# The single dense group of a tick moved from behind the prompt's scores to behind the transposes

## The reference, cut to what matters

```
h  = RMSNorm(x) * (1 + a1) + s1                       # modulation from silu(c) @ w_ada
q, k, v, hc, B, C, ga, gb = h @ w_in
beta = sigmoid(q.k / 8 + b_h)                          # 8 heads x 64
A[t,s] = beta[t,s] * prod_{s<j<t} (1 - beta[t,j])      # stick breaking, strictly causal
y  = B * dwconv3_causal(C * hc)
x  = x + g1 * (sigmoid(ga) * (A v @ w_att_out) + sigmoid(gb) * (y @ w_conv_out)) @ w_o
x  = x + g2 * relu(h2 @ w_mlp1)^2 @ w_mlp2             # h2 = RMSNorm(x) * (1 + a2) + s2
```

## Time and profile before

| | |
|---|---|
| median of 3 runs | 1692.57 us (1691.83 to 1693.04) |
| the profiled execution, its own time | 1693.47 us |
| its span, first to last instruction | 1691.7 us |
| mean granted clock of TensorE | 0.995 of full speed |
| TensorE busy, matmuls | 1648.2 us (97%) |
| VectorE busy | 870.2 us (51%) |
| GpSimd busy | 598.9 us (35%) |
| ScalarE busy | 371.2 us (22%) |
| middle stage | from 195.6 to 742.0 us of the span |

### The profile page before, as it was taken

The page is one execution under the profiler, slowest core; times in us unless marked ns, Lnnn a source line. Parts: engine busy times, 40 slices in busy tenths (PEclk is TensorE's granted clock), DMA queues, the critical chain, the costliest instruction groups (busy, mean ns, idle before and its releaser), DMA issues.

```text
span 1691.7 us, 29977 instructions
## 1 busy us (share of the span) xinstructions
PE 1648.2 (97%) x11976; PEld 1534.8 (91%) x11976; DVE 870.2 (51%) x1381; ACT 371.2 (22%) x702; POOL 598.9 (35%) x344
## 2 busy tenths in 40 slices
PE   6999999999999999999999999999999999999999
PEld 5898788878788788899999899999999999999998
DVE  5554364564554454438743865454554555454543
ACT  5344222222222222231111522020202011110200
POOL 0345143333343333313243143443443343343342
PEclk8999999999999999999999999999999999999999
DMA  9013346566566666425321011111111111111112
GB/s 379 27 51 100 139 163 225 201 200 215 198 213 222 207 220 230 150 103 204 127 102 50 26 50 51 50 38 51 51 38 51 50 39 49 50 45 44 51 39 102
DMA packets 71932, 194.63 MB, mean 115 GB/s; under 512 B 8018, under 2 KB 8147, under 8 KB 71795
## 3 DMA queue, kind: packets, MB, share of 16 engines
q1 hardware_dynamic: 67394, 178.62, 30.6%
q10 hardware_dynamic: 4400, 14.10, 2.2%
HBM read 174.26 MB, written 18.42 MB: 114 GB/s over the span
## 4 chain that ended last, share of the span: by engine, by line
PE 90%; DVE 3%; POOL 2%; DMA 1%; ACT 1%; issue 1%; SPq 1%; ACTq 0%; POOLq 0%; DVEq 0%
PE bank L655 78%; PE bank L805 2%; PE bank L780 2%; PE bank L793 2%; PE bank L829 2%; PE bank L853 1%; PE bank L685 1%; POOL wl L592 1%; DMA pre<-in_weights 1%; DVE h2L L1550 1%; POOL wh L590 1%; DVE hL L1269 1%; DVE sc L1582 1%; DMA ring<-in_cache_v 0%; DVE xt L1278 0%
## 5 line engine op out<-in xcount | busy, mean ns | idle before, releaser
L590 POOL TENSOR_TENSOR wh<-raw,zero 128x1024 fp32r<-128x1024 f32 x84 | 160.7, 1913 | 637.4 <-PE bank L655 637.4
L592 POOL TENSOR_TENSOR wl<-raw,wh 128x1024 fp32r<-128x1024 f32 x114 | 281.2, 2467 | 110.4 <-ACT wh L1069 103.8
L655 PE MATMUL bank<-hH,wh 128*128 128x352 f32 x832 | 277.2, 333 | 1.3 <-POOL wl L592 0.8
L655 PE MATMUL bank<-hL,wh 128*128 128x352 f32 x832 | 268.0, 322 | 0.0
L655 PE MATMUL bank<-hH,wl 128*128 128x352 f32 x832 | 267.5, 322 | 0.0
L655 PE MATMUL bank<-h2H,wh 128*128 128x352 f32 x768 | 249.2, 325 | 4.0 <-DVE h2L L1550 3.0
L655 PE MATMUL bank<-hidH,wh 128*128 128x352 f32 x768 | 247.7, 323 | 0.0
L655 PE MATMUL bank<-h2H,wl 128*128 128x352 f32 x768 | 246.9, 321 | 0.0
L655 PE MATMUL bank<-h2L,wh 128*128 128x352 f32 x768 | 246.7, 321 | 0.0
L655 PE MATMUL bank<-hidH,wl 128*128 128x352 f32 x768 | 246.3, 321 | 0.0
L655 PE MATMUL bank<-hidL,wh 128*128 128x352 f32 x768 | 246.1, 320 | 0.0
(11 more groups left out here) (177 smaller groups left out, 2571.3 us busy)
## 6 DMA issues: line engine op xcount, KB each, us to landing
raw<-in_weights SPq DMA_DIRECT2D x152, 512.0 KB, 3.5
ring<-in_cache_k SPq DMA_DIRECT2D x128, 256.0 KB, 3.9
ring<-in_cache_v SPq DMA_DIRECT2D x128, 256.0 KB, 3.6
pre<-in_weights SPq DMA_DIRECT2D x16, 512.0 KB, 15.9
gate_scratch<-gt ACTq DMA_DIRECT2D x14, 528.0 KB, 3.4
act<-gate_scratch SPq DMA_DIRECT2D x14, 528.0 KB, 5.1
xt<-in_xT SPq DMA_DIRECT2D x8, 528.0 KB, 6.9
act<-in_xT SPq DMA_DIRECT2D x8, 528.0 KB, 4.4
```

Source lines behind the costliest of these rows:

```text
L590: mark(pool.tensor_tensor(wh[u % 2][:, :], src[:, :], zero[:, 0:1].to_broadcast([P, 1024]), ALU.add))
L592: pool.tensor_tensor(wl[u % 2][:, :], src[:, :], wh[u % 2][:, :].bitcast(F32), ALU.subtract)\
L655: mm = pe.matmul(out, x, y, start=n == 0, stop=n == end)
```

## The change

The two conditions in `ticks()` are swapped. Group B is now there in every tick, and group A only where there are two. The number of groups in every tick and their order stay as they were; only in the 18 single ticks does the one group go from place A to place B, on TensorE as on the engines that read it or split its weights. The eviction and the split of such a tick move with it, and so do the keys by which loads are sorted.

```diff
@@ -219,10 +219,10 @@
     g, m, n = MIX0, 0, 16
     end = PLAN.phase["merge"][0]
     for k in range(TICKS):
-        if g < end:
+        if g < end and (k % 8 in (0, 1, 3, 4, 6) or k >= NSTEP):
             DENSE_A[k] = g
             g += 1
-        if g < end and (k % 8 in (0, 1, 3, 4, 6) or k >= NSTEP):
+        if g < end:
             DENSE_B[k] = g
             g += 1
         if k % 4 != 3 and m < NITEM:
```

## The result

The changed kernel takes 1726.19 us (median of 5 runs, 1723.49 to 1729.17) against 1692.57 us before: 2.0% slower, a ratio of 1.020 with a 95% interval of 1.0186 to 1.0214. The forecast was 1721.5 us with a range of 1711 to 1731. The profiled execution took 1724.13 us, with a span of 1722.3 us, 30.6 us more than before. Its mean granted clock is 0.989; before it was 0.995.

What follows compares the result with a forecast made beforehand. TensorE's matmuls were taken to bound the kernel, with time lost where its queue stands still. Costs of 36.6 less 9.4 plus 1.7 for the clock make 28.9 us: 1693.47 to 1722.4, less 0.9, 1721.5 us; range 1711 to 1731.

Steps and rivals of the forecast that it cites:

- Transposes held by VectorE's copy: Single ticks with sample turn: transposes wait for VectorE's sample copy behind the scans; 3.25 us each in six 512-key ticks.
- only the sigmoids count: Rival, chance 0.07: in single ticks VectorE's copy does not hold the transposes, only ScalarE's sigmoids do; 7.6 us, 1700 us.
- Ada turn held by the sigmoids: Single ticks: TensorE's ada turn waits for ScalarE's second sigmoid, 2.59 us after the start with 512 keys.
- The waiting in sum: Middle stage: single ticks cost 36.6 us gross, 9.4 of stalls before values and sample values go away, net 27.2.
- The clock: Middle stage: TensorE's bare stretches bring one more fall to half clock than now, net 1.7 us.
- add up to more than two or three: Sign in the changed trace: the forecast is wrong if windows at half clock exceed this count.
- The rival that gave the clock 13.6: Chance 0.13: the clock falls in most bare single ticks, eight falls at 1.7 us; 1733.4 us in all.
- Moved eviction and split: Single ticks: eviction and weight split go later with the group; priced at 0, between -1 and +2 us.

Runs made afterwards that it cites:

- the copy first: Changed kernel with VectorE taking modulation and sample copy ahead of 1 - beta and the scans in the 18 single ticks; 1699.61 us, ratio 1.0042 to the kernel before.
- filled kernel: Changed kernel plus 184 matmuls that nothing reads, put into the bare waits of 16 single ticks; 1714.53 us, ratio 1.0132 to the kernel before.
- fitted cut: Changed kernel with 2 to 7 of 8 row blocks before the transposes in 16 single ticks, the rest behind; 1683.56 us, again 1684.32 us.
- kernel with both remedies: Changed kernel with 3 of 8 row blocks in front in 16 single ticks, and modulation and sample copy ahead of VectorE's scans; 1686.97 us, ratio 0.9971.

## Why the prediction came out as it did

The direction, the place and the mechanism were right, and the time is in the range. Two terms of the sum were off in opposite directions, the clock the more, so that the nearness of the number is partly luck.

- *Transposes held by VectorE's copy.* Right. Predicted start with 512 keys 5.78, found 5.60; line 1388 is the releaser of 17.8 us; putting the copy first moved the start to 3.97. The rival "only the sigmoids count" is what that kernel makes true, and it measured 1699.6 where the rival's sum said 1700. In the changed kernel it is excluded.
- *Ada turn held by the sigmoids.* Right: predicted at 2.59 with 512 keys, found 222.53 - 220.05 = 2.48, since TensorE goes on 0.05 behind the sigmoid and not 0.15.
- *The waiting in sum.* Predicted 36.6 gross and 9.4 back, 27.2. By groups the changed kernel waits 18.8 + 12.8 + 1.6 = 33.2, and 8.9 + 0.5 + 1.5 = 10.9 went away, the last of them already in front of the transposes; that is 22.3. The filled kernel gives 22.5. So the sum was 4.9 too dear. Most of that can be found tick by tick. In the twelve ticks with a sample turn the transposes start earlier than worked out, 2.2 in sum: I set the sample copy 0.20 behind the end of the scans, and in tick 2 it starts at 225.22, 0.03 behind their end at 225.19. Tick 21 was priced by tick 45, whose old start is 5.68; its own was 6.54, another 0.9. The ada turns of ticks 15, 23, 39 and 47 wait 3.7 for 4.3. The rest is not broken down. Ticks 13 and 37 went the other way: without modulation their old start is 0.18 earlier, but the new one is not, which the prediction had assumed.
- *The clock.* The mis-sized term. The prediction counted by the one fall of before and took "one more than now net, 1.7", though it saw two bare stretches in a tick of 512 keys. The changed kernel has eight half-speed pieces. They cost 11.1 us in the profiled execution, 9.5 net of the 1.6 that the one fall cost before; the filled kernel puts it at 10.2 by times. The prediction had also named this as a sign of being wrong: windows at half clock that "add up to more than two or three". By that sign its clock term failed. The rival that gave the clock 13.6 was nearer in this term, though with its 27.2 us of waiting it comes out at 1733.4, too high.
- *Why the clock fell.* No single wait of TensorE in the stage is above 2.61 us, the clock went down and up six times, and with the waits filled it did not fall. The page that the prediction cites (the Trainium skill, TensorE: Matmul & The Clock Gate, "A second HAM failure mode: psum-queue depth-cycling") puts such a back and forth down to frequent short idle times between groups of matmuls. The traces agree with it.
- *The sum.* Waiting 22.3 and clock 9.5 make 31.8 of the 32.1 us by which the stage is longer. Behind the stage it is 1.5 us less: there the kernel before had one more fall (a granted clock of 0.53 from 968.0 to 971.6 us) and the changed one none. Together 30.6, the difference of the spans. Predicted 28.9, from 27.2 and 1.7: 4.9 too much waiting hid more than half of the 7.8 us that were missing for the clock.
- *Moved eviction and split.* Priced at 0. The double ticks of the changed kernel keep their lengths, 13.01 us in tick 9, 11.92 in tick 36, as before; only tick 35 is 1.6 shorter, which is the fall that it had before. Whether the order of single loads matters was not tried.

## What to carry to other kernels

A piece of work that fills a wait should be judged by what lies beside it on all other engines, not by what waits behind it: here 3.84 us of matmuls hid a chain of 5.6 us in front to save stalls of 0.5 us on average behind. If both places need cover, cut the piece to fit: 6 of 8 blocks in front in the ticks of 512 keys, 2 to 7 in the others (none in ticks 7 and 31), made the kernel 0.55% faster than the one before. When a change opens idle stretches on TensorE, add the falls of its clock to the sum; here they were a third of the loss, and filling the stretches with matmuls that nothing reads measured them.

## What was not expected of the hardware

- *Matmuls that nothing reads made a kernel faster.* 184 more matmuls, 10.2 us less time, on the same chip, with the granted clock of the stage at 1.00 in place of 0.98.
- *Run-to-run spread goes with the clock.* Runs of the changed kernel differ by 6.6 us, in step with the mean granted clock (0.990 to 0.986), and those of the kernel before by 6.7 (0.999 to 0.994). The filled kernel and the copy first lie within 1.7 us, but with 4 and 5 runs, and the fitted cut, with shorter idle stretches than the copy first, within 2.7 and 3.9 in its two sets of 5. So whether shorter stretches make runs agree is not shown.
- *A short scan of VectorE waits for the GpSimd product that it starts beside.* The sample's scan of 129 columns takes 0.49 us alone. In tick 2 of the changed kernel it starts at 226.37, beside the second of GpSimd's products of 512 columns, which ends at 224.15 + 3.35 = 227.50, and itself ends at 227.78. In the kernel before, 24 of its 32 runs in the stage have no product beside them and take 0.486 to 0.490; the other 8 start beside one and take 2.52 to 2.54. In both kernels every scan that starts beside a product ends 0.28 or 0.29 behind it, however much of the product was left (0.55 to 2.25). The Trainium skill (SBUF — State Buffer, "SBUF: two separate sides") says that a VectorE operation with two operands in SBUF and a GpSimd operation take one pair of ports in turn, each for its whole length. The rows agree with that. In the kernel with both remedies, 1 - beta of the sample (129 columns) took 1.25 beside a product, and the scan 1.40; in the fitted cut they took 0.33 and 1.40. So in both the copy of head 0 comes behind the product, and with both remedies it comes 1.2 later in the tick because the scans, and with them the product, begin 1.2 later.
